# A three-block network kernel: late heads' weight products moved, four-tile output units run by halves

## The reference

```python
x = x + rmsnorm(mamba2_mixer(rmsnorm(x)))              # "ssm", "ssm_out"
x = x + rmsnorm(swa_sink_mixer(rmsnorm(x)))            # "att", "att_out"
h = x + conv_pool_mixer(rmsnorm(x))                    # "cp", "cp_out"
h = h + (silu(hn @ w1) * (hn @ w3)) @ w2               # "up0", "down0"
h = h + hgrn2_mixer(rmsnorm(h))                        # "hg", "hg_out"
h = h + (silu(hn @ w1) * (hn @ w3)) @ w2               # "up1", "down1"
out = rmsnorm(h)

# swa_sink_mixer: q, k, v, gate = split(h @ w_in); per kv head (4) and query block (128)
p = softmax(q k^T / 8 with a band of 128 and a sink);  o = (p @ v) * silu(gate);  y = o @ w_out
# hgrn2_mixer: q, f_raw, i, g = split(h @ w_in); per head (8), f = lb + (1 - lb) * sigmoid(f_raw)
o = gated linear recurrence of (q, 1 - f, i, cumsum(log f));  y = (rms(o) * gn * silu(g)) @ w_out
```

## Time and profile before

| what | us |
|---|---|
| median of 3 runs | 1986.7 |
| lowest and highest run | 1977.89, 1986.87 |
| the profiled execution | 1993.01 |
| its span in the trace | 1991.0 |
| PE busy in it | 1884.4 (95%) |
| mean granted TensorE clock | 0.973 of full speed |

### The profile page before, as it was taken

One profiled execution on the slowest core, in us unless ns is written; L12 is line 12 of the kernel. 1 busy time (PEld: TensorE's weight loads), 2 busy tenths in 40 slices (PEclk: granted clock), 3 DMA queues, 4 the chain that ended last, 5 costly groups with the idle time before them and its releaser, 6 DMA issues.

```text
span 1991.0 us, 24975 instructions
## 1 busy us (share of the span) xinstructions
PE 1884.4 (95%) x9602; PEld 1488.4 (75%) x9602; DVE 1084.7 (54%) x1704; ACT 607.2 (30%) x1080; POOL 907.7 (46%) x910
## 2 busy tenths in 40 slices
PE   7899999897899887899999999999999799999997
PEld 5788878685677665557888888887777588888886
DVE  6888878835777756346333322147778663333212
ACT  5444445413233325032111100035567421111001
POOL 4444344355533146315555545553333265555552
PEclk9999999898999988999999999999999899999998
DMA  8676766485555354947888888896654388888884
GB/s 212 149 158 149 159 144 153 103 177 122 122 113 111 74 128 114 216 91 167 189 196 190 197 193 184 188 209 145 138 128 96 75 184 197 190 195 190 186 186 109
DMA packets 212838, 309.98 MB, mean 156 GB/s; under 512 B 22480, under 2 KB 166768, under 8 KB 212720
## 3 DMA queue, kind: packets, MB, share of 16 engines
q0 software_dynamic: 42624, 148.65, 44.0%
q1 hardware_dynamic: 165680, 154.34, 24.8%
q10 hardware_dynamic: 4416, 5.39, 1.1%
HBM read 153.18 MB, written 2.10 MB: 78 GB/s over the span
## 4 chain that ended last, share of the span: by engine, by line
PE 55%; DVE 2%; ACT 1%; ACTq 1%; issue 1%; POOL 0%; DMA 0%; DVEq 0%; POOLq 0%
PE gp L659 16%; PE gp L661 16%; PE gp L660 16%; PE mp L910 2%; PE mp L986 1%; ACTq L1337 1%; PE gp L630 1%; PE gp L629 1%; PE gp L628 1%; PE mp L1027 0%; PE mp L1036 0%; POOL sqsum L553 0%; DMA c_s<-c_a 0%; DVE h_sm L2160 0%; ACT L1121 0%
## 5 line engine op out<-in xcount | busy, mean ns | idle before, releaser
L573 POOL TENSOR_SCALAR wh<-stage 128x1024 fp32r<-128x1024 f32 (+2 forms) x298 | 346.4, 1162 | 926.3 <-PE gp L661 892.2
L659 PE MATMUL gp<-hh,wh 128*128 128x512 f32 x1544 | 620.5, 402 | 12.0 <-POOL wh L573 4.5
L660 PE MATMUL gp<-hh,wl 128*128 128x512 f32 x1544 | 603.9, 391 | 0.0
L661 PE MATMUL gp<-hl,wh 128*128 128x512 f32 x1480 | 578.9, 391 | 0.0
L659 PEld LDWEIGHTS gp<-hh,wh 128*128 128x128 f32 x1544 | 291.8, 189 | 80.6 <-issue 17.0
L579 POOL TENSOR_SCALAR wl<-stage 128x1024 fp32r<-128x1024 f32 (+2 forms) x296 | 350.8, 1185 | 0.0
L660 PEld LDWEIGHTS gp<-hh,wl 128*128 128x128 f32 x1544 | 291.9, 189 | 59.5 <-issue 1.2
L661 PEld LDWEIGHTS gp<-hl,wh 128*128 128x128 f32 x1480 | 279.0, 188 | 59.9
L582 POOL DMA_DIRECT2D wl<-stage x296 | 262.1, 885 | 94.1 <-POOL wl L579 83.4
L2055 DVE TENSOR_TENSOR val<-gp,rstd 128x512 f32<-128x512 f32 x44 | 30.4, 691 | 203.9 <-PE gp L661 203.9
L659 PE MATMUL gp<-f_h,wh 128*128 128x512 f32 x352 | 137.2, 390 | 0.0
(11 more groups left out here) (324 smaller groups left out, 2790.4 us busy)
## 6 DMA issues: line engine op xcount, KB each, us to landing
wl<-stage POOLq DMA_DIRECT2D x263, 512.0 KB, 5.3
stage<-ffn_w SPq DMA_DIRECT2D x120, 512.0 KB, 4.4
stage<-ssm_w_in SPq DMA_DIRECT2D x32, 512.0 KB, 4.9
stage<-hg_w_in SPq DMA_DIRECT2D x32, 512.0 KB, 4.5
stage<-ssm_w_in SPq DMA_DIRECT2D x32, 256.0 KB, 5.0
stage<-ssm_w_out SPq DMA_DIRECT2D x16, 512.0 KB, 4.6
stage<-att_w_in SPq DMA_DIRECT2D x16, 512.0 KB, 4.4
stage<-cp_w_in SPq DMA_DIRECT2D x12, 512.0 KB, 5.6
```

The costliest lines, as they stand in the source:

```text
L573: pool.tensor_scalar(wh[:, s, part], stage[:, s, part], 1.0, 1.0, ALU.mult, ALU.mult).then_inc(hi_done, 1)
L659: pe.matmul(bank[:, :], wvh[:, cols], hi(kk), start=start, stop=False)
L660: pe.matmul(bank[:, :], wvl[:, cols], hi(kk), start=False, stop=False)
L661: mm = pe.matmul(bank[:, :], wvh[:, cols], lo(kk), start=False, stop=stop)
```

## The change

Three things change. First, in `granules` a unit of more than two tiles is run by halves: all its tiles with the first half of the k's, a granule each, and then all with the second half. The number and the size of granules stay the same; the waits on `split_done` come with the first tile of each half, and each of the four banks is claimed within the first four granules.

Second, weight products move into the last rounds. In attention the last tile of group 3 (its second gate tile, 2 granules) is made in slot 0 of round 4, taken by VectorE in slot 1 and put through Silu in slot 2; round 3 has 8 granules, none behind slot 7. In hgrn the two gate tiles of pair 3 (4 granules) are made in slots 0, 2, 4 and 6 of round 4; round 3 has 12 granules, none in every fourth slot, and the tiles of pair 3 are taken in slots 1, 4, 6, 9, 12, 14, and 3 and 7 of the next round (`late_slots`), with Sigmoid, forget, Ln and scan moved along.

Third, output pieces are kept for the end: round 4 of attention issues 13 granules of `att_out` in place of 16, and round 4 of hgrn issues 9 of `hg_out` in place of 16, then one before output(7) and one before head_sum(7). A `load_ln()` is placed before the last head's root.

```diff
@@ -451,6 +451,17 @@
+        late_pair = HH // 2 - 1
+        late_slots = (1, 4, 6, 9, 12, 14, 19, 23)
+        def hg_slot(p, j):
+            return 16 * p + (late_slots[j] if p == late_pair else 2 * j + 1)
+        def hg_taken_at(slot):
+            return [(p, j) for p in range(HH // 2) for j in range(8) if hg_slot(p, j) == slot]
         def out_tile(name, k):
@@ -638,6 +649,30 @@
                     un = units[u]
+                    if len(un.tiles) > 2:
+                        for half in range(2):
+                            weights_whole(u, half)
+                            ka, kb = rows_of(u, half)
+                            for m, t in enumerate(un.tiles):
+                                if half == 0 and un.first and t >= 4:
+                                    pe.wait_ge(bank_read[t % 4], t // 4)
+                                cols = slice(m * P, (m + 1) * P)
+                                for k in range(ka, kb):
+                                    kk = un.k0 + k
+                                    if m == 0:
+                                        pe.wait_ge(split_done, split(kk) + 1)
+                                    wvh, wvl = weights_at(u, k)
+                                    bank = gp[t % 4]
+                                    pe.matmul(bank[:, :], wvh[:, cols], hi(kk), start=un.first and k == 0, stop=False)
+                                    pe.matmul(bank[:, :], wvl[:, cols], hi(kk), start=False, stop=False)
+                                    mm = pe.matmul(bank[:, :], wvh[:, cols], lo(kk), start=False,
+                                                   stop=un.last and k == un.kt - 1)
+                                if half == 0 and m == len(un.tiles) - 1:
+                                    mm.then_inc(first_used, 1)
+                                if half:
+                                    mm.then_inc(gemm_part, 1)
+                                yield
+                        continue
                     for m, t in enumerate(un.tiles):
@@ -880,9 +915,13 @@
                         if h < KVH:
-                            run(gran, (2, 1, 1, 1, 1, 1, 1, 1, 0, 1, 0)[k])
+                            late = h == KVH - 1
+                            run(gran, ((1, 1, 1, 1, 1, 1, 1, 1, 0, 0, 0) if late else
+                                       (2, 1, 1, 1, 1, 1, 1, 1, 0, 1, 0))[k])
+                        elif k == 0:
+                            run(gran)
                         else:
-                            run(gran_out, (2, 1, 1, 1, 1, 2, 2, 2, 2, 2, 0)[k])
+                            run(gran_out, (0, 1, 1, 1, 1, 1, 1, 1, 2, 2, 2)[k])
                         if h:
@@ -1040,7 +1079,10 @@
                         n, s = 2 * (p - 1) + k // 8, k % 8
-                        run(gran if p < HH // 2 else gran_out, 1)
+                        if p < late_pair or (p == late_pair and k % 4 < 3) or (p > late_pair and k in (0, 2, 4, 6)):
+                            run(gran, 1)
+                        elif p > late_pair and k > 6:
+                            run(gran_out, 1)
                         if p:
@@ -1319,8 +1363,12 @@
                                 exps(h - 1, k)
-                        if h < KVH and k in (7, 9):
-                            gate(h, (k - 7) // 2)
+                        if h < KVH and k == 7:
+                            gate(h, 0)
+                        if h < KVH - 1 and k == 9:
+                            gate(h, 1)
+                        if h == KVH and k == 2:
+                            gate(h - 1, 1)
                 post_norm_of(1, yo_a)
@@ -1472,16 +1520,17 @@
                                 head_high(n - 1)
-                        if p < HH // 2:
-                            if k % 2:
-                                take(p, k // 2)
-                            if k in (7, 9):
-                                log_f(p, (k - 7) // 2)
-                            if k >= 14:
-                                copy_vt(p, k - 14)
+                        for q, j in hg_taken_at(16 * p + k):
+                            take(q, j)
+                        for j in range(2 if p < HH // 2 else 0):
+                            if 16 * p + k == hg_slot(p, 2 + j) + 2:
+                                log_f(p, j)
+                        if p < HH // 2 and k >= 14:
+                            copy_vt(p, k - 14)
                     if p == 0:
                 head_square(HH - 1)
+                load_ln()
                 head_root(HH - 1)
@@ -1865,7 +1914,7 @@
                     tile_whole(dve, t)
-                    if h:
+                    if h and j < 3:
                         dve.wait_ge(qk_ready, h)
@@ -1912,10 +1961,12 @@
                                 low(split0["att"] + n, oh[:, n, :], ol[:, n, :])
-                        if h < KVH and k % 2 and k < 10:
+                        if h < KVH and k % 2 and k < (8 if h == KVH - 1 else 10):
                             take(h, k // 2)
-                            if h == 0 and k == 5:
-                                tables()
+                        if h == KVH and k == 1:
+                            take(h - 1, 4)
+                        if h == 0 and k == 5:
+                            tables()
                         if h < KVH and k == 10:
@@ -2218,13 +2269,13 @@
                             collect(m)
-                        if p < HH // 2:
-                            if k % 2:
-                                take(p, k // 2)
-                            if k in (6, 8):
-                                forget(p, (k - 6) // 2)
-                            if k in (8, 10):
-                                scan(p, (k - 8) // 2)
+                        for q, j in hg_taken_at(16 * p + k):
+                            take(q, j)
+                        for j in range(2 if p < HH // 2 else 0):
+                            if 16 * p + k == hg_slot(p, 2 + j) + 1:
+                                forget(p, j)
+                            if 16 * p + k == hg_slot(p, 2 + j) + 3:
+                                scan(p, j)
                     if p == 0:
```

## The result

| | before | after |
|---|---|---|
| median, us | 1986.92 (6 runs) | 1969.96 (6 runs) |
| lowest and highest, us | 1977.89, 1991.13 | 1967.37, 1974.2 |
| ratio after/before | | 0.9922, 95% interval 0.9908 to 0.9936 |
| the profiled execution's span, us | 1991.0 | 1967.3 |

The change gains 17.0 us, 0.85%; forecast were 15.1 us. The page of the changed kernel, to be read against the earlier trace rows: PE has the same 9602 matmuls and is busy for 12.2 us less, as fewer of them run at the low clock (mean granted clock 0.980, before 0.973); the other 11.5 us of the shorter span are waits that are gone.

A forecast was written before the change was run, and what follows sets the result against it. PE, busy 1884.4 of 1991.0 us, was taken as the bound, so only its waits and low-clock time could be regained. hgrn 11.2, attention 0 and cp_out 3.9 sum to 15.1 us: median 1986.7 to 1971.6 us, range 1962 to 1983.

The forecast's parts named there:

- hgrn, 11.2 us forecast: Round 3, both heads of round 4 and the tail together: 137.5 us against 148.7, 11.2 us gained (bounds 5 and 16).
- Round 3: In hgrn, four granules of 12 fewer: 64.2 us falls to 53.4, plus 1.2 us of waiting, 54.6 us.
- The second head: In hgrn's round 4, 21 more matmuls, a Silu and both engines full: 22.1 us becomes 24.6 us (bounds 22.1 and 27).
- Attention, 0 forecast: In attention, 5.1 us lost at the end against 5.4 us gained: 0 us (bounds 4 lost, 5.4 gained).
- cp_out, 3.9 forecast: At cp_out, halves remove waits of 0.58 and 2.27 us and half of 2.5 us: 3.9 us gained (bounds 1 and 4.1).
- Weights, 0.5 us for each place: First two-tile unit's second half of weights may land late, 7.6 us against 8.1: 0.5 us per place, at worst 4 each.
- The mark for "wrong" that came true: Sign that the prediction is wrong: the first two-tile unit of `hg_out` or `att_out` waits for `wl`.
- heads become the bound: Rival: DVE and ScalarE need 3 to 4 us more in hgrn's round 3 and both heads; 1981 us, chance 0.16.
- All covered: Rival: no new wait anywhere in the kernel, 25.5 us gained, 1961 us; chance 0.10.
- nothing gained: Rival: moved matmuls only move the waits, which reappear in rounds 3; 0 to 3 us gained, 1985 us; chance 0.08.
- the slower case: Rival: the thinned attention rounds run at 1.2 GHz, PE at low clock for all of round 4; 1999 us, chance 0.04.
- the table switches: Rival: six table loads on chains in attention and hgrn hold ScalarE twice as long, 7.7 us more; 1979 us, chance 0.04.

The follow-up runs named there:

- control: The changed kernel measured again with no edit; median 1969.64 us, ratio 0.9919 to the kernel before.
- e3: The changed kernel with attention's schedule of before put back, run by halves and hgrn moves kept; median 1967.83 us, ratio 0.9908 to the kernel before.
- e7: The changed kernel with cp_out's units run tile by tile, as before, not by halves; median 1977.0 us, ratio 0.9962 to the kernel before.
- e8: The changed kernel with the eighth granule of attention's round 3 back in slot 9 instead of slot 7; median 1974.3 us, ratio 0.9937.
- e10: The changed kernel with 16 output granules instead of 13 in attention's round 4, none kept for the end; median 1970.3 us, ratio 0.9927.
- e4: The changed kernel with moved Silus in round 4 later: attention's in slot 8, not 2; hgrn's in 11 and 15, not 3 and 7; median 1973.65 us.
- e12: e3 with both moved Silus of hgrn together in slot 7 of round 4, sharing one pair of table loads; median 1968.17 us, ratio 0.9913.
- e2: The kernel before with the hgrn moves alone, no run by halves, attention as before; median 1979.6 us, ratio 0.9958 to the kernel before.
- e1: The kernel before with only the run by halves of four-tile units added; median 1968.48 us, ratio 0.9906 to the kernel before.

## Why the prediction was right, and where its terms were off

The median of 1969.96 us lies 1.6 us under the forecast of 1971.6, inside its own range. The waits that were to go went; that the sum came so near is partly luck. Term by term:

- *hgrn, 11.2 us forecast.* Measured 10.7 us by the prediction's windows, 10.9 by the table, 9.6 in the control, and 8.5 to 11.1 in e3, e7, e8 and e10, whose hgrn code is the same. Right as a sum by luck, from two errors that cancel, +2.8 and -3.1 us. Round 3 was put at 54.6 us with 1.2 us of waiting; it took 57.4, and 58.6 in the control: the two waits of 2.4 us, slow matmuls behind them, and VectorE instructions caught by POOL. The second head was put at 24.6 us because both engines would be full; it took 21.5: PE's busy time rose to 20.85 us, as reckoned, but fitted into the head's old length. The first Silu was charged 0.8 us and cost 1.5 (e4, e12). The first head (22.7 against 23.2) and the tail (35.6 against 35.9) were right, as was the cover of the last head's wait.
- *Attention, 0 forecast.* Measured 1.0 us gained, 0.7 in the control. Its working holds in its parts: the last value product was to end 3.1 us later, and *b* and *c* together grew by 3.0 to 4.0 us over the five profiles with this attention; the end was to win 5.4 us less 9 matmuls of 2.0 us, 3.4, and *d* fell by 4.0 (2.9 against e2). The gap of 4.3 us was there with 4.38, the clock fell behind it, and round 3 did not get shorter. The 1.5 us charged for the slow rotations were 0.6 in two profiles and 1.5 to 1.8 in five. The comparison with hgrn was misread, though: there the matmuls of the kernel before ran at half clock ahead of the gap of 4.43 us (the sum of 2.07 us in the earlier trace rows is one), so that gap did not send the clock down. And of VectorE's waits in round 3, 6.0 us were for the Exp, but 0.7 us for ScalarE's `a_oh`, which the prediction left out.
- *cp_out, 3.9 forecast.* Measured 4.9, of which 3.4 are sure and 1.4 depend on whether the clock had fallen. That the stretched subtraction may fall elsewhere was the reason for 3.9; it went away.
- *Weights, 0.5 us for each place.* The fear was right in its mechanism: the split weights of the first two-tile unit of `hg_out` land 1.04 to 1.19 us late in every profile with halves and hgrn's kept pieces. In attention no such wait came.
- *The mark for "wrong" that came true:* that unit of `hg_out` does wait for `wl`. At 1.16 us against the 0.5 charged it did not move the sum.

*What the prediction missed* is whose gain it is. It worked out one sum for three edits and never one for the halves alone. e1 shows that they give the whole of it, 17.6 us, in an edit that moves no work from one round to another. The moves, worth 6.5 us without the halves (e2), are on top of them worth some -4.6 us in attention and +1.0 to +3.6 us in hgrn. Its own sum held the cue: in attention 5.1 us lost against 5.4 us gained, and the gain could be had without the loss, since the four granules of k 6 that the halves free (2.7 us) come close to the 2.81 us of the wait alone.

The rivals: "heads become the bound" (1981 us) came true in round 3 alone. "All covered" fell, and "nothing gained" too, though in attention the moved matmuls did only move the waits. The clock's mean from 671.6 to 714 us, round 4 of attention, was 0.96, as in the kernel before, so the slower case had nothing behind it. For the table switches, every load in the lines above is followed by the next instruction after 0.01 to 0.02 us; a drain of 1380 ns, which the Trainium skill (ScalarE: Activation LUTs, What ACT_TABLE_LOAD costs) adds to each, shows in none of them; the measurement decides. A pair of loads with its Silu holds ScalarE for 3.2 us, of which 1.5 us reached the head (*h6* of e12).

No version was found that the medians tell from e1. Those of e1, e3 and e12 lie within 0.7 us; by stages e12 has the shortest hgrn and an attention as short as e1's, 4.4 us in all under e1's, and its median doesn't bear that out. The change's order of round 3 gives 57.2 to 58.6 us in four profiles and 59.6 to 59.8 in six. The six have two or three VectorE instructions caught, the four one or none; that this makes the whole 2.4 us is argued from the rows, since no run sets POOL's time alone. What stays open is why the clock differs behind equal waits.

## What to carry to other kernels

When a change has several edits, work out what each gives alone: two that fill the same wait do not add up, and here the simplest, the order of a unit's row blocks, had the whole gain. Work kept for the end pays where the rounds have it in excess and a chain stands bare behind them (hgrn), and costs where a chain sets the length of the rounds, for then it leaves holes there and comes on top at the end (attention). Where effects are smaller than the spread of a run, measure stages between the same instructions, with a control.

## What the runs showed of the hardware

- A VectorE instruction of 0.41 us with both inputs in SBUF takes 1.20 to 1.26 us when it meets a pass of POOL, and a subtraction of 0.69 us took 3.04 us against two passes in a row; a copy out of PSUM is not held. Which instruction is caught is set by when PE frees a half of the weights: at full clock POOL's pass came at 20.4 us into the head and caught three, behind a clock of 0.76 it came at 21.9 to 22.1 us and caught one, and the head was 2.4 us shorter. A stage can so be shorter behind a lower clock.
- The same gap does not always bring the same clock: behind 2.26 or 2.27 us of waiting at the same place the first matmul took 0.80 us in one profile and 0.50 us in two, with 1.4 us of difference to the end of the stage. Behind one and the same gap of 4.4 us four rotations took 2.6 us in two profiles and 3.5 to 3.8 in five; behind one of 2.02 us they took 3.58 us. Behind the same waits of 1.15 and 1.26 us the clock of the next stretch was 0.65 to 0.76 in five profiles and 1.00 in five.
